# A mixture-of-experts kernel: the heads of its two expert stages rewired, the second stage's down weights loaded in another order

## What is computed

```python
def hier_moe(n, w_grp, b_grp, w_exp, b_exp, w1, w3, w2):
    g_idx = argmax(x @ w_grp + b_grp)              # 1 of 4 groups
    e_logits = (x @ w_exp + b_exp)[its group]      # 8 experts in it
    top_v, top_i = lax.top_k(e_logits, 2)
    gate = softmax(top_v) * g_prob                 # g_prob: softmax of the groups
    expert_id = g_idx * 8 + top_i                  # 32 experts
    ...
    def expert_block(args):                        # tokens sorted by expert, in blocks
        xb = x[toks]
        return (silu(xb @ w1[e]) * (xb @ w3[e])) @ w2[e]
    ...                                            # out[token] += weight * y
```

## Time and profile before

| | |
|---|---|
| three runs, us | 1571.43, 1572.54, 1575.5; median 1572.54 |
| profiled execution, span, us | 1574.9 |
| PE busy | 1353.3 us (86%) |
| PEld busy | 876.2 us (56%) |
| DVE busy | 689.2 us (44%) |
| ACT, POOL busy | 247.8 us (16%), 80.0 us (5%) |
| large transfers | 521.30 MB on SP's queue, 81.8% of 16 engines |
| stage 1 / stage 2, start to end, us of the span | 167.5 to 664 / 1124 to the end |

### The profile page before, as it was taken

One profiled execution on the slowest core, in us unless ns is written; L12 is line 12 of the kernel. 1 busy time (PEld: TensorE's weight loads), 2 busy tenths in 40 slices (PEclk: granted clock), 3 DMA queues, 4 the chain that ended last, 5 costly groups with the idle time before them and its releaser, 6 DMA issues. The chain is left out here.

```text
span 1574.9 us, 27743 instructions
## 1 busy us (share of the span) xinstructions
PE 1353.3 (86%) x11912; PEld 876.2 (56%) x11912; DVE 689.2 (44%) x1844; ACT 247.8 (16%) x505; POOL 80.0 (5%) x125
## 2 busy tenths in 40 slices
PE   9999998997978789899999999999896676666665
PEld 8655554553455566588767748886453343333332
DVE  4634664322223343427687536652562332332333
ACT  2322330110001111233223113230200000000000
POOL 2401000000000000030000200100000000000000
PEclk9999999999988999999999999999998878887887
DMA  9965899999999999877522454476999999999996
GB/s 336 270 232 191 335 426 429 424 425 427 427 430 425 426 425 427 352 251 280 200 93 106 148 174 160 165 284 257 381 393 429 429 430 429 431 430 430 430 427 252
DMA packets 94023, 528.20 MB, mean 335 GB/s; under 512 B 8282, under 2 KB 10610, under 8 KB 67684
## 3 DMA queue, kind: packets, MB, share of 16 engines
q1 hardware_dynamic: 88792, 521.30, 81.8%
q0 software_dynamic: 2624, 5.32, 1.4%
q10 hardware_dynamic: 2508, 0.17, 0.1%
HBM read 525.70 MB, written 1.07 MB: 334 GB/s over the span
## 5 line engine op out<-in xcount | busy, mean ns | idle before, releaser
L1568 PE MATMUL ps<-weight_ring,e_xT 128*32 128x256 f32 x3456 | 247.8, 449 | 131.4 <-DMA weight_ring<-in_w_up_dram 89.2
L1568 PEld LDWEIGHTS ps<-weight_ring,e_xT 128*32 128x32 f32 x3456 | 137.0, 128 | 237.6 <-issue 192.7
L1848 DVE TENSOR_TENSOR e_g<-e_act_g,ps 128x128 f32<-128x128 f32 x64 | 24.8, 388 | 263.5 <-ACT e_act_g L1655 262.3
L1846 DVE TENSOR_TENSOR e_act_g<-e_act_g,ps 128x128 f32<-128x128 f32 x32 | 9.2, 286 | 236.2 <-ACT e_act_g L1655 236.2
L1655 ACT ACTIVATE e_act_g<-ps 128x128 f32<-128x128 f32 x64 | 17.8, 278 | 565.5 <-PE ps L1568 558.3
L1568 PE MATMUL ps<-expert_set,e_xT 128*32 128x256 f32 x640 | 51.3, 491 | 42.5 <-DMA expert_set<-in_w_up_dram 42.5
L1598 PE MATMUL ps<-weight_ring,e_gT 128*32 128x256 f32 x1344 | 82.6, 387 | 4.2 <-DVE e_gT L1852 2.0
L2369 PE MATMUL ps<-expert_set,weight_ring 128*128 128x256 f32 x384 | 84.2, 379 | 0.0
L2369 PEld LDWEIGHTS ps<-expert_set,weight_ring 128*128 128x128 f32 x384 | 73.0, 190 | 9.9
L1532 PE MATMUL ps<-e_y,e_routing 32*128 32x256 f32 x1024 | 74.3, 404 | 2.1 <-DVE e_y L1880 1.5
L1524 PE MATMUL ps<-e_n,e_Gt 128*32 128x256 f32 x1056 | 70.9, 385 | 3.8 <-DVE e_Gt L1795 2.0
(11 more groups left out here) (614 smaller groups left out, 1945.4 us busy)
## 6 DMA issues: line engine op xcount, KB each, us to landing
weight_ring<-in_expert_w_dram SPq DMA_DIRECT2D x80, 2048.0 KB, 23.0
weight_ring<-in_w_in_dram SPq DMA_DIRECT2D x26, 2048.0 KB, 9.6
weight_ring<-in_w_down_dram SPq DMA_DIRECT2D x20, 2048.0 KB, 38.8
weight_ring<-in_w_gate_dram SPq DMA_DIRECT2D x19, 2048.0 KB, 32.9
weight_ring<-in_w_up_dram SPq DMA_DIRECT2D x19, 2048.0 KB, 37.4
weight_ring<-in_w_ada_dram SPq DMA_DIRECT2D x12, 2048.0 KB, 12.6
expert_set<-in_w_gate_dram SPq DMA_DIRECT2D x10, 2048.0 KB, 33.4
expert_set<-in_w_up_dram SPq DMA_DIRECT2D x10, 2048.0 KB, 37.9
```

What stands on the lines that cost most here:

```text
L1568: mm = pe.matmul(ps[32 * j:32 * j + 32, 4, 0:256].rearrange("p (w f) -> p w f", w=2), xT[:, k, :], w13[:, :, k, j * P:(j + 1) * P], start= ...
L1848: dve.tensor_tensor(g[:], spread(act_g[:]), spread(ps[:, 4, P:2 * P]), ALU.mult).then_inc(s_g, 1)
```

## The change

Both stages' heads are rewired, and SP's order in stage 2.

- DVE makes expert 0's mask (`hot0`) directly: logit of group 0 at least the best group's, logit of expert 0 at least the second best of the first eight. Two matmuls of one and two columns give its positions (`first_positions`), a copy and two compares its one-hot, and the gather follows; `take_x(0)` comes before the rest of the mask work.
- The positions of all experts (`positions`, four matmuls) move into the ups of expert 0, behind their first half.
- The one-hots of experts 1 and 2 come straight from positions (`early_one_hot`); slots, gates and `wide` (`slots_and_gates`) follow after expert 1's x is taken.
- The transposes of `wide` move from behind the down of expert 0 to behind the gather of expert 1; `GwT` and `Gw2` are no longer cleared, and `s_Gw` counts one less.
- The residual goes, in stage 1, from behind the ups of expert 0 to behind the ups of expert 1; in stage 2 it is cut in three pieces placed around the first positions and the gather. The dummy products change from 11 and 4 calls to 2, 6 and 8 in stage 1, and from 4 and 4 to 3 in stage 2.
- `DOWN_AFTER` for stage 2: after the ups of expert 3 comes down 6, after 5 down 5, and after i from 6 on down i+1, each with the wait for its buffer.

```diff
-        DOWN_AFTER.update((i, i) for i in range(11 if SETS == 2 else 5, STATIC))
+        DOWN_AFTER.update(((i, i) for i in range(11, STATIC)) if SETS == 2 else
+                          ((i, {3: 6, 5: 5}.get(i, i + 1)) for i in range(3, STATIC - 1) if i != 4))
...
-            if x is not None:
-                x.pe_transposes(pe)
-                keep_busy(c, pe, 7, 11)
-            else:
-                residual()
-                keep_busy(c, pe, 7, 4)
...
+            def first_positions():
+                pe.wait_ge(s_hot0, 1)
+                pe.wait_ge(s_iota, 1)
+                pe.matmul(pos0_ps, tri[:], hot0, start=True, stop=False, skip_group_check=True)
+                pe.matmul(pos0_ps[:, 1:2], c.ones[:], hot0[:, 0:1], start=False, stop=True, skip_group_check=True).then_inc(s_pos0, 1)
...
+            if x is not None:
+                x.pe_transposes(pe)
+                keep_busy(c, pe, 7, 2)
+            else:
+                residual((0, 1))
+            first_positions()
+            if x is not None:
+                keep_busy(c, pe, 7, 6)
+            else:
+                residual((2,))
             pe.wait_ge(s_n, 2)
             pe.wait_ge(s_Gt, 1)
             gather()
-            keep_busy(c, pe, 7, 4)
+            if x is not None:
+                keep_busy(c, pe, 7, 8)
+            else:
+                residual((3,))
+                keep_busy(c, pe, 7, 3)
...
                     if known and i == 0 and k == KD // 2 - 1:
                         mm.then_inc(s_uph, 1)
+                        positions()
                 mm.then_inc(s_up, 1)
                 first, second = known and i == 0, known and i == 1
-                if first:
-                    if x is not None:
-                        x.pe_taken(pe)
-                        residual()
-                elif x is not None and known:
+                if x is not None and second:
+                    x.pe_taken(pe)
+                    residual()
+                if x is not None and known and not first:
                     x.pe_early(pe, i)
                 pe.wait_ge(s_Gt, i + 2)
                 pe.wait_ge(s_y, i + 1)
                 gather()
+                if second:
+                    pe.wait_ge(s_slot, 1)
+                    for v in range(8):
+                        mm = pe.transpose(ps[:, 6 + v // 4, (v % 4) * P:(v % 4 + 1) * P], wide[:, v, :], c.ident[:])
+                    mm.then_inc(s_rows, 1)
                 if not first:
-                    pe.wait_ge(s_Gw, i + 1)
+                    pe.wait_ge(s_Gw, i)
                     combine()
...
+            for tt in range(TT):
+                ins = dve.max(top8[:, tt, :], el[:, tt, 0:EPG])
+            link(ins)
+            link(dve.tensor_tensor(slot[:, 1, :], el[:, :, 0], top8[:, :, 1], ALU.is_ge))
+            link(dve.tensor_tensor(hot0, gl[:, :, 0], gm[:], ALU.is_ge))
+            dve.tensor_tensor(hot0, hot0, slot[:, 1, :], ALU.mult).then_inc(s_hot0, 1)
...
                 dve.wait_ge(s_gather, i + 2)
...
+                begin = isinstance(i, int) and i == 0
+                if begin:
+                    early_one_hot(2)
+                    slots_and_gates()
+                    gated_y()
                     rows()
+                    step(VO - 4, dve.tensor_scalar(slot[:], slot[:], -2.0 * SLOTS, None, ALU.add))
+                else:
```

More of the change, by code:

```diff
@@ L1344, in moe @@
         slot = sb("slot", [P, 2, TT])
+        hot0, pos0 = slot[:, 0, :], gate[:, 1, :]
         over = etmp
@@ L1500, in _, with residual, positions @@
         def _(pe):
-            def residual():
-                for m in range(4):
+            def residual(ms=range(4)):
+                for m in ms:
                     mm = pe.matmul(ps[:, m, :].rearrange("p (t n) -> p t n", t=TT), c.ident[:], h[:, :, m * 256:(m + 1) * 256],
                               start=True, stop=False, skip_group_check=True)
-                mm.then_inc(s_comb, 1)
-            if x is not None:
-                x.pe_transposes(pe)
-                keep_busy(c, pe, 7, 11)
-            else:
-                residual()
-                keep_busy(c, pe, 7, 4)
[L1514 to L1519, removed]
+                if ms[-1] == 3:
+                    mm.then_inc(s_comb, 1)
+            def first_positions():
[3 more added lines that the diff above has]
+                pe.matmul(pos0_ps[:, 1:2], c.ones[:], hot0[:, 0:1], start=False, stop=True, skip_group_check=True).then_inc(s_pos0, 1)
+            def positions():
+                pe.wait_ge(s_hot, 1)
+                pe.matmul(pos_ps, tri[:], both[:].rearrange("p t e -> p (t e)"), start=True, stop=False, skip_group_check=True)
+                pe.matmul(pos_ps[:, NE:2 * NE], c.ones[:], both[:, 0, :], start=False, stop=True, skip_group_check=True).then_inc(s_pos, 1)
+                pe.matmul(tot_ps, c.ones[:], both[:, 0, :], start=True, stop=False, skip_group_check=True)
+                pe.matmul(tot_ps, c.ones[:], both[:, 1, :], start=False, stop=True, skip_group_check=True).then_inc(s_tot, 1)
             def gather():
@@ L1744, in _ @@
             link(ins)
+            dve.wait_ge(s_pos0, 1)
+            link(dve.tensor_copy(pos0, pos0_ps))
+            for tt in range(TT):
+                ins = dve.tensor_scalar(Gt[:, tt, :], ie[:], pos0[:, tt:tt + 1], hot0[:, tt:tt + 1], ALU.is_equal, ALU.mult)
+            ins.then_inc(s_Gt, 1)
             by_group = lambda v: v[:].rearrange("p t (g e) -> p (t g) e", g=NG)
@@ L1798, in _ @@
-            dve.wait_ge(s_ve, 1)
-            link(dve.tensor_scalar(gate[:, 0, :], gate[:, 1, :], 1.0, None, ALU.add))
-            link(dve.tensor_tensor(gate[:, 0, :], gate[:, 0, :], gprob[:], ALU.mult))
-            link(dve.reciprocal(gate[:, 0, :], gate[:, 0, :]))
-            link(dve.tensor_tensor(gate[:, 1, :], gate[:, 0, :], gate[:, 1, :], ALU.mult))
-            if last:
-                dve.wait_ge(s_comb, 1)
-                dve.wait_ge(s_n, 2)
-            for v in range(8):
-                src = (slot, gate)[v // 4][:, (v // 2) % 2, v % 2:v % 2 + 1]
-                ins = dve.tensor_copy(wide[:, v, :], src.to_broadcast([P, P]))
@@ L1877, in expert @@
                     block_table()
-                if mod is not None:
-                    dve.wait_ge(s_down, i + 1)
-                    dve.tensor_tensor(y[:], ps[:, 5, 0:256], gate_m[:], ALU.mult).then_inc(s_y, 1)
+                if not begin:
+                    gated_y()
             if mod is not None:
```

108 lines of the change are left out of this document (55 added, 53 removed).

## The result

| | before | after |
|---|---|---|
| device time, median of 13 executions each, us | 1575.33 | 1580.13 |
| lowest and highest, us | 1571.43, 1577.52 | 1576.21, 1582.16 |
| profiled execution, span, us | 1574.9 | 1576.3 |
| time after / time before | | 1.0032, 95% interval 1.0023 to 1.0041 |

The changed kernel is slower by 4.8 us, 0.3%. The forecast was +1.1 us by its sum. Device time is some 1.7 us more than the span, so the execution profiled of the changed kernel (1578.04) is one of its shorter ones; its trace is shown first, longer ones stand among the experiments.

A forecast was written before the change was run, and what follows sets the result against it. The weight stream was taken to bound both stages, with PE's order setting load issue early in stage 1. Stage 1's 4.1 us less stage 2's 3.0 gave +1.1 on the median 1572.54, forecast as 1573.5, range 1567 to 1578.

The forecast's parts named there:

- What bounds the kernel: Both expert stages: the weight stream; an edit to the heads pays only by removing idle holes, 4.1 and 2.2 us.
- The first ups: Stage 1 head: ups of expert 0 start at 174.6 instead of 176.48, 1.85 us earlier (bounds 0 and 2.6).
- Expert 0: Stage 1, from ups of expert 0 to ups of expert 1: 8.4 us instead of 11.8, 3.4 less.
- Expert 1: Stage 1, from its ups to its down: 15.3 us instead of 5.6, 9.7 more, as moved work lands there.
- The clock in stage 1: PE's 3.7 us pause between transposes and combine lowers its clock: 1.5 us more (bounds 0 and 1.7), 6.0 late in all.
- the clock stays low: Rival, chance 0.10: stage 1 has further stretches at 1.2 GHz, 1.7 us each; three give 1578.7; decides from the third on.
- Stage 2: Shorter head issues expert 4's load at 1142.7 instead of 1148.70, closing the hole at 1146: -3.0 us (bounds 0 and -3.0).
- a clock that falls costs nothing: Stage 2, ahead of expert 5's load: down 6 adds 4.9 us to the queue, less 3.0, enough to cover a slow clock.
- The stream takes it all: Rival, chance 0.18: PE only looks full, residual and pause are absorbed, both holes shrink: -4.9 us, 1567.7.
- The pause does not reach the clock: Rival, chance 0.19: PE's pause in stage 1 does not slow its clock; stage 1 is 2.6 us later, 1572.1.
- The ups do not start earlier: Rival, chance 0.07: fillers or DVE hold PE until 176.5; stage 1 loses 5.9 us, stage 2 still closes its hole, 1575.4.
- The likeliest case: The forecast itself, chance 0.46: stage 1 4.1 us later, stage 2 3.0 us shorter, giving 1573.5.

The follow-up runs named there:

- each repair: Two edits to the changed kernel: transposes ahead of stage 1's residual (1574.42 us), then also stage 2's gate rows between its first two down loads (1572.51 us).
- the rows in time: Old stage 1 with new stage 2, its four gate-row DMAs issued between the first and second down load instead of behind both: 1572.13 us.
- the run with the old places: Old stage 1 with stage 2's new head, but each down load back behind the ups of its own expert: 1578.44 us.
- the filled pause: The changed kernel with 28 dummy PE passes behind the transposes of stage 1, where PE stood still 3.76 us: 1577.00 us.

## Why the prediction was wrong, point by point

**What bounds the kernel** was right: an edit counted only where it changed the holes of the weight stream, and each repair moved the time with the hole it closed. The sum slipped by 0.1, as 1.1 on 1572.54 is 1573.6; nothing hangs on it.

**The first ups** were right: forecast 174.6, measured 174.59, 174.74 and 174.43 in three traces of the changed kernel. In the first it was 176.29, because 16 transposes ahead of the head ran at half clock. **Expert 0**: 8.4 forecast, 176.29 to 184.74 is 8.45. **Expert 1**: 15.3 without the clock; 184.74 to 200.54 is 15.8, of which 0.94 is the slow combine. PE's lateness at the ups of expert 2 (forecast 6.0) was 5.5, 5.9, 6.7 and 7.4 us in the four traces, and the two holes came where they were foreseen.

**The clock in stage 1** is the first step that failed, in size. It was put at 1.5 us with 1.7 as its bound, from one pause of the trace of before. In the four traces it cost, over combine, down, gates and ups of expert 2 at their full-clock durations (1.15, 1.93, 3.62, 3.66), 1.6, 1.4, 3.3 and 4.5 us (the last: 0.94 + 1.71 + 0.17 + 1.69), 2.7 in the mean. The first two bear out the 1.5; the other two go the way of the rival "the clock stays low", which had 0.10: 1.8 and 3.0 us more than the 1.5, where the rival takes 1.7 for each further low stretch. "It decides from the third on" was too late a mark, as the stream had only 1.9 us to spare and each further us went into the hole in full. The rest of that step held: expert 5's load, forecast six late, was issued 7.2 us later than before (219.72) in the mean of five traces with the new stage 1 (5.5 to 8.4), and less the 1.9 that is 5.3, the very delay of stage 2. Traces with the new stage 1 put the start of stage 2 at 1126.6 to 1130.7, 1129.3 in the mean of five; six with the old one at 1124.0 in the mean. That is 5.3 us later, 6.3 by the medians, where 4.1 was forecast with 5.9 as the upper bound. The trace of before had more to say on the clock than the pauses that were read: in its stage 2 a pause of only 2.03 us was followed by a slow gather and a slow down (1.07 and 1.93 at full clock).

```profile
1139.12 1.49 PE L1524 MATMUL ps<-e_n,e_Gt 128*32 128x256 f32 x16 [2.03 <-DVE e_Gt L1795]
1141.21 2.81 PE L1598 MATMUL ps<-weight_ring,e_gT 128*32 128x256 f32 x32 [0.60 <-issue]
```

**Stage 2** is the second, and here a wait was missed. The ups of expert 0 come 6.25 us behind the start of the stage (forecast 6.6), but those of expert 1 only 1.7 us earlier than before against the start (19.04 against 20.74), where 6.0 was forecast: the wait for the gate rows, which the prediction had at nothing, takes it. With the rows in time they come 6.3 us earlier (14.44), so that part of the chain was right, and the 1.7 us that PE was to wait for DVE's `y` are 1.94 there. The prediction asked for the new waits that the diff writes, not for old ones that had always been met in time and that an earlier engine now meets first. The hole in front of expert 4's load closed all the same, since down 6 stands ahead of it (the run with the old places shows that hole open). But expert 5's load, forecast "nearly as today", is issued 36.4 us behind the start of the stage instead of 32.0: the 1.9 us that down 6 was to add to the queue (4.9 - 3.0) were gone, and "a clock that falls costs nothing" was wrong. By the medians, the stage gives 3.4 us with the rows in time, about the 3.0 of the forecast, and 0.3 without.

**The sum.** +4.8 (+5.7 when run again) against +1.1. By the medians of the stages, stage 1 accounts for 2.2 us of the difference (6.3 against 4.1) and stage 2 for 2.7 (-0.3 against -3.0). The traces give 5.3 - 2.5 = 2.8 of the 4.8 to 5.7 us; the rest, most of it in stage 2, is seen in the medians alone, and its cause stays open. The absolute time was off by 6.6 us: the other 2.8 are the base, since the three runs at hand (median 1572.54) lay below the median of the larger set (1575.33). The profiled execution was compared with them by its span; with the 1.7 us around the span it lay 4.1, not 2.4, above them, which was a warning.

**The rivals.** "The stream takes it all" is refuted: every trace of the changed kernel has holes where PE came late and the loads with it. The Trainium skill ("Perfetto Trace Analysis", Identifying the Most-Contended Engine) judges TensorE's headroom by its share of peak FLOPs and by weight-load busy; by the latter that rival would have won. The trace does not agree, at least not here, where PE's place in its own order sets the issue of loads: 21.3 of 42 us of weight loads, and the lateness came out as holes of 3.6 and 0.9 us. "The pause does not reach the clock" is refuted by the filled pause. "The ups do not start earlier" was so in one trace of four and was not the cause. The likeliest case failed by the two errors, clock and missed wait. The range (up to 1578) was missed by 2.1 us, less than the 2.8 of the base: from the median of the larger set it would have reached 1580.8 and held the result, so the base decided that miss. What the sum did not have is the case in which both errors come together, though both heads had spent their reserve.

## What to carry over

When an edit makes an engine early somewhere, list every wait that it will meet from there on, the ones that never cost anything included, and look up when each releaser lands; a small load queued behind large ones is such a releaser. Where a chain's reserve against the next transfer is spent, price each stretch behind a new pause of TensorE at the low clock as a direct loss, several of them, and put the case with all of them into the range. Move dependent work to where another engine's long step covers it (here the transposes ahead of the residual, which took back the loss of stage 1), and let a one-execution pair of traces prove the mechanism but not the size.

## What the runs showed of the hardware that was not expected

TensorE's clock behind the same pause of 3.76 us was not the same from execution to execution: the combine took 1.88 to 2.09 us in the four traces of the changed kernel (1.15 at 2.4 GHz), the down 2.41, 2.60, 2.84 and 3.64 (1.93). The ups of expert 2, which start 9 to 12 us behind that combine, were partly at 1.2 GHz in five of ten traces with the new stage 1 (5.15 to 5.35 us against 3.66), also in one whose pauses ahead were all under 0.7 us, and in none of six with the old stage 1. What sets it off there is open; no run was made for it.

Four DMAs of 32 KB issued on SP's queue behind two of 2 MB landed 11.4 us after their issue (medians of 11.3 to 11.7 in 13 traces), and 6.8 us when they went between the two (6.8 to 7.0 in three).
